# Two-layer hybrid decoder trunk on one core: key norms per token, attention in another order, feature tiles six and two, conformer tiles first

## What is computed

```python
# RWKV-7, even layer: 8 heads of 64 features
kk = heads(k * k_k)
kk = kk / jnp.maximum(jnp.linalg.norm(kk, axis=-1, keepdims=True), 1e-12)
...
# cross-attention
q = (h @ wq).reshape(bsz, seqlen, XA_HEADS, XA_HEAD_DIM)
s = jnp.einsum('bthd,bmhd->bhtm', q, k) * (XA_HEAD_DIM ** -0.5)
pr = jax.nn.softmax(s, axis=-1)
o = jnp.einsum('bhtm,bmhd->bthd', pr, v).reshape(bsz, seqlen, D_MODEL)
return o @ wo
...
# the mixers' output projection; odd layer: conformer (512), mamba (1024)
h = _layer_norm(DN_ALPHA * h + jnp.concatenate([y_a, y_b], axis=-1) @ w_out, ...)
```

## Time and profile before

| | |
|---|---|
| median of 3 executions | 1776.17 us (1776.01 to 1777.78) |
| the profiled execution's own time | 1773.76 us |
| its span in the trace | 1772.0 us |
| mean granted TensorE clock | 0.975 of full speed |
| TensorE busy | 1667.2 us, 94% |
| VectorE busy | 1016.5 us, 57% |
| ScalarE busy | 745.0 us, 42% |

### The profile page before, as it was taken

One profiled execution on the slowest core, in us unless ns is written; L12 is line 12 of the kernel. 1 busy time (PEld: TensorE's weight loads), 2 busy tenths in 40 slices (PEclk: granted clock), 3 DMA queues, 4 the chain that ended last, 5 costly groups with the idle time before them and its releaser, 6 DMA issues.

```text
span 1772.0 us, 26805 instructions
## 1 busy us (share of the span) xinstructions
PE 1667.2 (94%) x11018; PEld 1389.7 (78%) x11018; DVE 1016.5 (57%) x1276; ACT 745.0 (42%) x990; POOL 142.7 (8%) x160
## 2 busy tenths in 40 slices
PE   7998998989899999999999989799998999999996
PEld 6777897878787888888877767788787788888885
DVE  4689564664666543434488974655646755434345
ACT  4544543363525232323267854634534442324231
POOL 5110110000000000000016630000000000000000
PEclk9999999999899999999999999899999999999998
DMA  5220002344022323333332320143530233323331
GB/s 196 70 84 26 3 4 97 131 131 129 26 95 84 100 90 107 91 100 119 95 119 72 95 72 24 42 161 109 154 95 13 95 108 95 101 89 107 92 122 60
DMA packets 41161, 159.73 MB, mean 90 GB/s; under 512 B 4560, under 2 KB 4688, under 8 KB 39632
## 3 DMA queue, kind: packets, MB, share of 16 engines
q1 hardware_dynamic: 41040, 158.03, 28.4%
HBM read 153.81 MB, written 4.19 MB: 89 GB/s over the span
## 4 chain that ended last, share of the span: by engine, by line
PE 77%; DVE 15%; ACT 5%; issue 2%; POOL 1%; DMA 0%; SPq 0%; DVEq 0%; ACTq 0%; POOLq 0%
PE bank L588 23%; PE bank L590 23%; PE bank L589 22%; DVE w_lo L1712 2%; DVE h L1728 1%; DVE sconv L1728 1%; DVE act_lo L1725 1%; PE bank L752 1%; DVE nbh L1773 1%; PE bank L1092 1%; ACT w_hi L1223 1%; DVE bank L1728 1%; PE bank L771 1%; PE bank L765 1%; DVE lnst L2041 1%
## 5 line engine op out<-in xcount | busy, mean ns | idle before, releaser
L1712 DVE TENSOR_TENSOR w_lo<-w_raw,w_hi 128x1024 fp32r<-128x1024 f32 x263 | 326.2, 1241 | 303.2 <-ACT w_hi L1223 300.3
L588 PE MATMUL bank<-act_lo,w_hi 128*128 128x512 f32 x1048 | 416.6, 397 | 30.5 <-DVE w_lo L1712 18.7
L1223 ACT ACTIVATE w_hi<-w_raw 128x1024 fp32r<-128x1024 f32 x263 | 278.9, 1061 | 364.1 <-PE bank L590 348.2
L589 PE MATMUL bank<-act_hi,w_lo 128*128 128x512 f32 x1048 | 411.2, 392 | 0.0
L590 PE MATMUL bank<-act_hi,w_hi 128*128 128x512 f32 x1048 | 411.0, 392 | 0.0
L588 PEld LDWEIGHTS bank<-act_lo,w_hi 128*128 128x128 f32 x1048 | 198.6, 189 | 80.1 <-issue 22.0
L589 PEld LDWEIGHTS bank<-act_hi,w_lo 128*128 128x128 f32 x1048 | 198.6, 190 | 42.2 <-issue 1.7
L590 PEld LDWEIGHTS bank<-act_hi,w_hi 128*128 128x128 f32 x1048 | 198.7, 190 | 42.1
L588 PE MATMUL bank<-w_lo,aux_hi 128*128 128x512 f32 x576 | 225.2, 391 | 5.3 <-DVE act_lo L1725 5.3
L590 PE MATMUL bank<-w_hi,aux_hi 128*128 128x512 f32 x576 | 224.8, 390 | 0.0
L589 PE MATMUL bank<-w_hi,aux_lo 128*128 128x512 f32 x576 | 224.7, 390 | 0.0
...
## 6 DMA issues: line engine op xcount, KB each, us to landing
w_raw<-weights SPq DMA_DIRECT2D x263, 512.0 KB, 3.6
...
```

The source lines that it names most:

```text
L588: pe.matmul(o, whi, xlo, start=first, stop=False)
L589: pe.matmul(o, wlo, xhi, start=False, stop=False)
L1223: act.activation(w_hi[:, s], w_raw[:, s], ACT.Copy).then_inc(S("w_hi_done"), 1)
L1712: dve.tensor_tensor(w_lo[:, s], w_raw[:, s], f(w_hi[:, s]), ALU.subtract).then_inc(S("w_split"), 1)
```

## The change

Eight edits, of which 1 to 7 move or replace work; the eighth merges three counters of SyncE's loads and stores of `h` into one.

1. Key norms per token. `norms(b)` now makes eight matmuls with the squared keys as the stationary operand and two columns of `bdones`, so one bank holds 128 tokens x 16 norms. Root, maximum and reciprocal act on 128x16 (`norm_scales`), and `norms_back(b)` spreads the scales over each head's 64 partitions by sixteen matmuls; VectorE multiplies from PSUM.
2. A `turn` in `TILES` gives the second half of the first output projection other banks than its first half.
3. The load of the memory tokens goes from SyncE's queue to ScalarE's, and `memory(l)` stands earlier.
4. While `h` is normalised before the attention, the split of key chunk 2 stands at token tile 2 instead of 0 (ScalarE) and 1 (VectorE).
5. Six feature tiles, first half of the values' steps, two feature tiles, the rest.
6. Attention: score tiles of the first head pair before the last two query chunks; then probabilities, scores and values in turn; the output projection waits tile by tile.
7. Odd layer: conformer norms one head pair earlier, gates and low halves of the conformer tiles inside the loop, both roots behind it; the output projection takes the tiles in their own order (conformer first), and the two spreadings stand at its tiles 2 and 6. Its second half reuses the first half's banks.

```diff
-        TILES += [IN0[0], IN0[1], ("rdec0", 2), ("ra0", 2), IN0[2], ("rss0", 2), IN0[3], ("rbon0", 2), IN0[4],
-                  IN0[5], ("rdec1", 2), ("ra1", 2), IN0[6], ("rss1", 2), IN0[7], ("rprod0", 10), ("rtok0", 8), ("rw0", 2),
+        TILES += [IN0[0], IN0[1], ("rdec0", 2), ("ra0", 2), IN0[2], ("rss0", 1), IN0[3], ("rnb0", 2), ("rbon0", 2), IN0[4],
+                  IN0[5], ("rdec1", 2), ("ra1", 2), IN0[6], ("rss1", 1), ("in0_7", 2), ("rnb1", 2), ("in0_7", 2), ("rprod0", 10), ("rtok0", 8), ("rw0", 2),
...
-        TILES += [("out0", 4), ("rback", 4), ("out0", 4)]
+        TILES += [("out0", 4), ("rback", 4), ("turn", 4), ("out0", 4)]
...
-            TILES += [("crb", 1)] * (_h == 0) + [("rsum", 1)] * (_h in (1, 5)) + [("rbc0", 1)] * (_h == 6)
-            TILES += [("free rsum", 0)] * (_h == 6)
-        TILES += [("out1", 4), ("rbc1", 1), ("free rsum", 1), ("out1", 4)]
-    TILES += [(f"k{_l}", 8), (f"lnt{_l}_0", 8), (f"v{_l}", 4), (f"q{_l}", 8), (f"s{_l}", 8),
-              (f"pt{_l}_0", 4), (f"pt{_l}_1", 4), (f"pv{_l}_0", 4), (f"pv{_l}_1", 4), (f"wo{_l}", 8),
+            TILES += [("crb", 1)] * (_h == 0) + [("rsum", 1)] * (_h in (1, 5))
+        TILES += [("out1", 4), ("rbc0", 1), ("free rsum", 0), ("rbc1", 1), ("free rsum", 1), ("out1", 4)]
+    TILES += [(f"k{_l}", 8), (f"lnt{_l}_0", 6), (f"v{_l}", 2), (f"lnt{_l}_0", 2), (f"v{_l}", 2), (f"q{_l}", 6), (f"s{_l}", 2),
+              (f"q{_l}", 1), (f"s{_l}", 2), (f"q{_l}", 1), (f"pt{_l}_0", 2), (f"s{_l}", 2), (f"pt{_l}_0", 2), (f"s{_l}", 2),
+              (f"pv{_l}_0", 2), (f"pt{_l}_1", 2), (f"pv{_l}_0", 1), (f"pt{_l}_1", 2), (f"pv{_l}_0", 1), (f"pv{_l}_1", 4), (f"wo{_l}", 8),
               (f"lnt{_l}_1", 8)]
...
+    if _name == "turn":
+        _free.rotate(-_count)
+        continue
...
             def norms(b):
+
                 pe.wait_ge(S("r_kksq"), b + 1)
+                o = take(f"rss{b}", 0)
                 for j in range(2):
-                    o = take(f"rss{b}", j)
-                    pe.matmul(o[:], bdones[:], s_fwd[:, j], start=True, stop=True).then_inc(S("mixer_mm"), 1)
+                    for m in range(NT):
+                        at = 2 * (NT * j + m)
+                        last = pe.matmul(o[:, at:at + 2], s_fwd[:, j, m * P:m * P + P], bdones[:, 0:P:RD], start=True,
+                                         stop=True)
+                last.then_inc(S("mixer_mm"), 1)
+
+            def norms_back(b):
+
+                pe.wait_ge(S("r_norm"), b + 1)
+                for j in range(2):
+                    o = take(f"rnb{b}", j)
+                    for m in range(NT):
+                        for q in range(2):
+                            at = 16 * b + 2 * (NT * j + m) + q
+                            last = pe.matmul(o[RD * q:RD * q + RD, m * P:m * P + P],
+                                             small[:, at:at + 1].to_broadcast([P, RD]), ident[:], start=True, stop=True)
+                    last.then_inc(S("mixer_mm"), 1)
...
+                project(7, {2: lambda: norms_back(1)})
...
+                to_features(l, 0, 0, 6)
+                token_major(f"v{l}", 2, KD, memv[0], memv[1], between={4: lambda: to_features(l, 0, 6, 8)})
...
+                feature_major(f"q{l}", 8, act_hi, act_lo, T, ready=lambda k: of(f"lnt{l}_0", "_out", k + 1),
+                              between={6: lambda: scores_between(0), 7: lambda: scores_between(2)})
+                probs_to_memory(0, 0, 2)
+                scores(1, 0, 2)
+                probs_to_memory(0, 2, 4)
+                scores(1, 2, 4)
+                pe.wait_ge(*out_sem(f"v{l}", 4))
+                values(0, 0)
+                probs_to_memory(1, 0, 2)
+                values(0, 1, 0, 1)
+                probs_to_memory(1, 2, 4)
+                values(0, 1, 1, 2)
+                values(1, 0)
+                values(1, 1)
+                token_major(f"wo{l}", NT, KD, act_hi, act_lo, ready=lambda k: of(f"pv{l}_{k // 4}", "_out", k % 4 + 1),
+                            by_token=True)
...
-                    if n % 3 == 0 and t == 0:
+                    if n % 3 == 0 and t == 2:
...
+                if i == 2:
+                    memory_in(0)
+                if i == 4:
                     memory(0)
...
                 if hp == 5:
-                    root(0)
-                if hp >= 5:
-                    conf_gate(hp - 5)
+                    conf_gate(0)
+                    conf_gate(1)
+                if hp == 6:
+                    conf_gate(2)
+                    conf_gate(3)
+            root(0)
+            root(1)
+            split(FIRST["out1"] + 1 + W_SLOTS)
...
-            def normalised(b, part):
-
-                dve.wait_ge(S("rss_out"), 2 * b + part + 1)
-                step(dve.tensor_scalar(NBH[b][:, part], NBH[b][:, part], 1e-12, None, ALU.max))
-                step(dve.reciprocal(NBH[b][:, part], NBH[b][:, part]))
-                step(tt(NBT[b][:, part], NBT[b][:, part], NBH[b][:, part], MUL))
+            def norm_scales(b):
+
+                dve.wait_ge(S("rss_out"), b + 1)
+                norm = small[:, 16 * b:16 * b + 16]
+                step(dve.tensor_scalar(norm, norm, 1e-12, None, ALU.max))
+                done(dve.reciprocal(norm, norm), "r_norm")
+
+            def normalised(b):
+
+                for j in range(2):
+                    dve.wait_ge(*made("rnb", 2 * b + j + 1))
+                    done(tt(NBT[b][:, j], NBT[b][:, j], bank(f"rnb{b}", j)[:], MUL), "rnb_out")
...
-                            if final % 3 == 0 and t == 1:
-                                split(FIRST[f"k{final // 3}"] + W_SLOTS)
                             if t:
                                 normalise(final, t - 1)
+                            if final % 3 == 0 and t == 2:
+                                split(FIRST[f"k{final // 3}"] + W_SLOTS)
...
+                    if i == 5:
+                        row_max(0)
+                        row_max(1)
+                    if i == 6:
+                        probs(0)
+                        probs(1)
+                        row_max(2)
+                        row_max(3)
+                probs(2)
+                probs(3)
+                row_max(4)
+                probs_lo(0, 0, 2)
+                row_max(5)
+                probs_lo(0, 2, 4)
+                row_max(6)
+                row_max(7)
+                probs(4)
+                probs(5)
+                split(FIRST[f"wo{l}"] + W_SLOTS)
+                probs(6)
+                probs(7)
+                values_lo(0, 0, 2)
+                probs_lo(1, 0, 2)
+                values_lo(0, 2, 3)
+                probs_lo(1, 2, 4)
+                values_lo(0, 3, 4)
+                values_lo(1, 0, 4)
...
-                if hp in (1, 2):
-                    conf_norm(2 * hp - 2, 2 * hp)
-                if hp == 5:
-                    rstd(0)
+                if hp in (0, 1):
+                    conf_norm(2 * hp, 2 * hp + 2)
+                if hp >= 6:
+                    conf_lo(2 * hp - 12)
+                    conf_lo(2 * hp - 11)
+            rstd(0)
+            split(FIRST["out1"] + 1 + W_SLOTS)
             rms(0)
             mix_lo(4, 8)
-            conf_lo(0)
-            conf_lo(1)
-            conf_lo(2)
-            split(FIRST["out1"] + 1 + W_SLOTS)
             rstd(1)
-            conf_lo(3)
             rms(1)
```

197 lines of the change are left out of this document (95 added, 102 removed).

## The result

| | before | changed |
|---|---|---|
| median | 1776.09 us (1775.75 to 1777.78, 4 runs) | 1745.55 us (1740.32 to 1746.64, 4 runs) |
| profiled execution, span | 1773.76, 1772.0 us | 1744.99, 1743.3 us |
| mean granted clock | 0.975 | 0.984 |

The ratio is 0.982 (95% interval 0.9807 to 0.9832), a gain of 30.5 us. Forecast were 1744 us and a gain of 32.

What follows compares the result with a forecast made beforehand. TensorE, busy 1667.2 of 1772.0 us, was taken as the bound, with gains in its waits and low-clock stretches. Terms A to G summed to -32.1, so 1776.2 - 32 = 1744 us, range 1732 to 1762.

Steps and rivals of the forecast that it cites:

- G: Odd output projection taking conformer tiles first: starts 5.3 us earlier, part given back in new waits; -2.0 us (-5 to +1).
- A: Key norms per token in the even mixer, both groups: -4.0 us (-6.7 to +1.3), spreading priced at 3.1 us per group.
- B: Second half of the first output projection: other banks remove the 2.56 us wait and slow clock behind it; -3.6 us.
- C: First key projection weights, chunk 2 split later: layer 0 wins 0.5, layer 1 loses 1.5; +1.0 us (-2 to +3).
- D: Feature tiles in two lots: the values' 2.65 us wait for banks goes in both layers; -6.5 us (-7.1 to -5).
- E: Attention in new order, both layers: softmax runs under projections, fewer TensorE waits; -10 us (-13 to -5).
- F: Conformer norms one head pair earlier: the 4.02 us wait for a copy and slow head pair go; -7.0 us.
- a sign against it: Even mixer's key norms: the prediction expected no wait over 1 us before the masked products' ninth tile (L718).
- P: Start of key projection chunk 0, from which the prediction counted when chunks 2 and 3 come.
- the first rival: Waits move to VectorE's queue, chiefly in the attention: only -15 us, so 1761 us; chance 22%.
- The clock rival: Many short waits keep TensorE at 1.2 GHz through each attention: +40 us, so 1780 us, slower than before; chance 4%.
- The second: All of it comes: spreading at half price, no attention wait over 1 us; -43 us, so 1733 us; chance 16%.

## Why the prediction was right, and where it was not

The time was forecast at 1744 and is 1745.55, the gain at 32 and is 30.5. The mechanisms were right except in G; that the sum came within 1.5 us is partly luck. In the table of places A and B won 2.3 us more than forecast, C and G together 2.5 less, and 2.2 were lost at the start, where no term was; the two profiles are 28.8 us apart, the medians 30.5. The steps one by one; measured are the stretches above.

| term | forecast | measured | by |
|---|---|---|---|
| A | -4.0 | -5.5 (-4.1 to -6.0) | table; edit 1 taken back |
| B | -3.6 | -4.4 to -4.6 | table; no turn |
| C | +1.0 | -0.3 and +1.9, together +1.5; taking it back gives -3.7 | table; edit 4 taken back |
| D | -6.5 | -6.8 | edit 5 taken back |
| E | -10 | about -9.8 (-6.8 to -13.7) | edit 6 taken back |
| F | -7.0 | -6.4 to -7.1 | table; norms late |
| G | -2.0 | 0.0 in the two profiles, +0.5 to +1.4 | table; order taken back |

**A.** The price of the spreading was mis-sized: 1.89 us per group, not 3.1. The row of L1092 was the wrong neighbour; its matmuls add into a bank and read other operands, and even grouped by half the new ones take 2.49. The rule of the Trainium skill (TensorE: Matmul & The Clock Gate, "Part 3: Packing small matmuls"), that matmuls on different column tiles run at once, was right in direction: alternating halves take 0.76 of the grouped time. The halving that I had derived from it did not come. In exchange there is a wait that I did not see, 1.29 us at 137.92, over the 1 us that the prediction had named as a sign against it: VectorE's small reciprocal stands behind two convolutions, and TensorE's spreading needs it. With these, the ninth tile's wait is 0.53 (forecast 0.5) and ends on the same copy, and the clock of the stretch is 1.00.

**B.** The mechanism was right; what the wait cost beyond its idle time was 1.8 to 1.9 us, not 1.0.

**C.** Two waits, as forecast: 1.33 (forecast 1.0 to 1.4) and chunk 3 at P + 12.9 (12.3 to 13.0). Layer 1 lost 1.9, layer 0 won 0.3. What the sum against the kernel before hid is that layer 0's gain belonged to edit 3. Costing each edit against the program in which it stands, not against the old one, would have shown 3.7 us to be had.

**D.** As forecast in size. The price is made up a little otherwise: 2.66 + 0.24 of idle time in each layer, where I had 2.65 alone, and 0.5 more in each, where I had 0.6 of low clock; in the run the clock there was not low.

**E.** The waits came nearly as stepped through: 0.62 (0.7), twice 0.32 (0.35), 3.03 (3.2); the 0.4 did not come. Of the 3.03, 2.1 us were the order of VectorE's queue, as the run with that order changed shows. From the end of the last query chunk to the output projection are 470.99 - 443.33 = 27.7 us in layer 0 and 24.9 in layer 1 (forecast 26), 37.9 and 36.7 before.

**F.** As forecast: the wait is gone, and the slow head pair with it.

**G.** The start came as worked out: 1124.61 in the changed trace is 1146.2 on the old scale. What was mis-sized is what is given back. I had 2.3 at the ninth tile and 2.0 at the half; measured 2.33 and 2.28, but also 0.86 at the fifth tile, and the first spreading (0.8), which had stood ahead of the projection and now stands in it. From the start to the second half are 1166.35 - 1124.61 = 41.7 us, against 1187.97 - 1151.50 = 36.5 before: 5.5 of waits and 0.8 of spreading, less slow work. That takes all of 5.3 back. The 0.99 for the last square sum is a new wait too; it sits before the start.

**The rivals.** Waits did move to VectorE's queue (3.03, 2.33, 0.86), as the first rival had it, but the waits that the sum did not have are 1.29, 0.99 and 0.86, some 3 us, not 17. The clock rival did not come true in any profile. The second, everything at its low end, was met in A by half; E, G and C stayed far from its -13, -5 and -1.
